# A tenth buffer for expert weights, loaded during the scan, in place of most of the room for GpSimd's DMA descriptors

## The chip, the cores and the metric

The kernel runs as one launch on one core of a Trainium2 chip. The metric is the device time of that launch in microseconds (us). TensorE is called PE, VectorE DVE, ScalarE ACT, GpSimd POOL and SyncE SP.

## The reference

Two blocks follow each other on 256 tokens of width 1024, all in float32. The first block has two layers, each of a mixer (retention, dilated attention, spatial gating) and a gated FFN. The second block is a state-space scan with a pooling branch and then a mixture of 32 experts (4 groups of 8), of which each token uses two. Cut to what matters here:

```
def hybrid_layer(...):                                   # twice
    z = jnp.matmul(rms_norm(x, g_mix_pre), w_in)
    y = concatenate([retention, dilated attention, spatial_gating(gelu(gu), gelu(gv), w_s, b_s)])
    x = x + rms_norm(jnp.matmul(y, w_out), g_mix_post)
    gate, up = jnp.split(jnp.matmul(rms_norm(x, g_ffn_pre), w_gate_up), [FFN_HIDDEN], axis=-1)
    return x + rms_norm(jnp.matmul(jax.nn.silu(gate) * up, w_down), g_ffn_post)

# second block: modulate, ssd_scan, pooling branch, post_norm, then
def hier_moe(h, lp):
    lg = hf @ lp['w_rg'] + lp['b_rg']                    # router: groups
    le = jnp.einsum('td,gde->tge', hf, lp['w_re']) ...   # router: experts of a group
    def swiglu(xb, wg, wu, wd):
        return (jax.nn.silu(xb @ wg) * (xb @ wu)) @ wd   # for all 32 experts' tokens
```

## The kernel before, in words

Each engine has one instruction stream written out by hand, and semaphores order the streams. `at(...)` gives the semaphore and count at which a named event has happened.

**Weights of the dense stages.** Weights stream through `ring` in units, which SP loads in order (`load_to`, `load`). The ring has four slots of a megabyte in the first block and two in the second. A unit is cut into quarters. Each quarter is split into a high part (ACT, `split_hi`) and a low part, made by DVE or by POOL (`lo_to`, one TENSOR_TENSOR into `split_r`); PE then multiplies with both. There are four places for split quarters, so ACT starts quarter k when PE has finished quarter k-4. In the gate/up stage of the first block's FFN (22 units, m = 0 to 21, two quarters each) DVE makes the low parts of first quarters and POOL those of second quarters. SP may load a new unit into a slot once the high and low parts of what lay there are made.

**POOL's loop in gate/up.** For each m it runs `lo_to` for the quarters ahead, then `low(m)` (the low part of the activations, after ACT has made the high part of unit m), and in the first layer one step of the generator `small_loads`. That generator issues small DMA loads for the second block; its last ten steps (m = 7 to 16) load the router's weights into WR: for each of two halves of the rows, one load from `w_router_group_2` and four from `w_router_expert_2`. In each of the ten, every one of 128 partitions has four separate runs (of 16 or 32 bytes).

**POOL's other loads.** At the start: positions, six small rows, then `conv_w`, `b_ada`, GCOL and BCOL (`ln1_g_2`, `ln1_b_2`, two runs in each partition), BP (`b_ada_2`, four runs in each partition), and then `cst1` (1344 KB). In each layer: WS (`w_s`, four runs of 512 bytes in each partition), then two rows of gains broadcast over the partitions. Later the context CX, with two runs in each partition.

**Room for POOL's descriptors.** Loads that POOL issues have lists (descriptors) that POOL writes into SBUF. The program sets aside bytes of each partition for them, 16384 by default; `kernel()` builds with the default.

**Experts.** The experts' stage streams 96 matrices of 2 MB (gate, up and down of 32 experts), numbered k = 0 to 95. They go through nine places of SLOT = 4096 floats per partition (`expert_slots`: four in `arena`, four in `ring`, one in `rows`); matrix k takes place k mod 9. Pairs of experts p share six matrices: two gates, two ups, two downs. Matrices 0 to 7 are issued by ACT as the dense stages let go of the memory, 8 and on by SP (`expert_loads`), in order; from k = 9 each waits until PE has finished with matrix k-9. Some (2, 9, 10 and 92 to 95) are loaded in two halves. Between the scan and this stage lie the gates, branches a and b and `out2`.

The lines touched are 317 to 375 (allocation and semaphores), 534 to 596 (places and loads of experts), 991 (PE's wait for the router's weights), 1768 to 1810 (ACT's expert loads), 2766 to 2772 (`small_loads`), 2790 (WS), 2888 (BP), 2990 to 3022 (SP's loads) and 3088 (`kernel()`).

Of the kernel before, what the change touches and what calls it, by code (L numbers as in the profile page):

```python
# [291 lines left out]
def program(nc, A, out):  # L292
    st = ExitStack()
    with st:
# [24 lines left out]
        posi = sb("posi", [P, 2], I32)  # L319
        rope = sb("rope", [P, 2, 2, 32])  # L320
        rt = rows[:, 4 * D:4 * D + P].rearrange("p (a b c) -> p a b c", a=2, b=2)
        posf = sb("posf", [P, 2])
        cnt = sb("cnt", [P, 1], I32)
        AR = 26624
        ar_at = nc.sbuf_base + (-nc.sbuf_base) % 32
# [46 lines left out]
        s_last = {e: sem(f"last_{e}") for e in ("dve", "pool")}  # L372
        s_w = [[sem(f"expert{i}") for i in range(9)]] + [[sem(f"expert{r}_{i}") for i in range(8)] for r in range(1, ROUNDS)]
        s_second = [sem(f"expert_second{i}") for i in range(4)]
        s_round = [None] + [{e: sem(f"round{r}_{e}") for e in ("pe", "act", "dve")} for r in range(1, ROUNDS)]
# [55 lines left out]
        GT2 = view(23424, 2, 512)  # L431
        JUNK = view(25472, 2, 512)
        ACH = view(4096, 22, 256, rounded=True)
        ACL = view(9728, 22, 256, rounded=True)
# [53 lines left out]
        def blocks8(a0, a1, rounded=False):  # L488
# [43 lines left out]
        SEL, RK, CW, RS, CM, CB = R(400, 2, 32), R(464, 2, 32), R(528, 2, 32), R(592, 2, 32), R(656, 1, 2), R(660, 2, 36)  # L532
        expert_slots = [ar[:, 18432:18432 + SLOT], ar[:, 22528:22528 + SLOT], ar[:, 10240:10240 + SLOT], ar[:, 14336:14336 + SLOT],
                        ring[:, 0:SLOT], ring[:, SLOT:2 * SLOT], ring[:, 2 * SLOT:3 * SLOT], ring[:, 3 * SLOT:4 * SLOT], rows[:, D:D + SLOT]]

        slot_for = lambda r, k: expert_slots[k % (9 if r == 0 else 8)]

# [49 lines left out]

        in_halves = lambda r, k: r == 0 and (k in (2, 9, 10) or k >= 92)

        def half_load(e, k, q):  # L590

            p, j = divmod(k, 6)
            o = slot_for(0, k)[:, q * RAW:(q + 1) * RAW]
            w = A["w_expert_up_2" if j < 4 else "w_expert_down_2"][0, 2 * p + j % 2]
            src = w.rearrange("(q p k) n -> q p (k n)", q=2, k=4)[q] if j < 4 else w.rearrange("(p q k) n -> q p (k n)", q=2, k=2)[q]
            e.dma_start(o, src).then_inc(*landed(s_second[k % 4] if q else s_w[0][k % 9], ("ew", 0, k, q)))

        def tensor(t):  # L600
# [346 lines left out]
            def convolution():  # L947
# [17 lines left out]
                for m in range(24):  # L965
                    c = CHUNKS[m]
                    if m < 3:
                        finished(m + 1)
                    else:
                        bk = take(("cv", m), ("conv", m))  # L970
                        chunk(bk if c < 20 else bk[:, 256:512], q0 + 1 + m, 0 if c < 20 else 1, 2).then_inc(*sig(s_mm, ("cv", m), ("split_done", q0 + 1 + m)))
                    if m >= 2:
                        to_tokens(m - 2)
                    if m == 1:
                        bk = take(("dtt",), ("dtraw",))
                        t.wait_ge(*at("cv", -1, "kept"))
                        for i in range(4):
                            made = t.transpose(bk[:, i * 64:(i + 1) * 64], DTT[:, tok(i)], ident[0:64, 0:64])
                        made.then_inc(*sig(s_turn, ("dtt",)))
                    if m == 10:  # L980
                        dt_sums()
                    if m == 11:
                        bk = take(("acst",), ("acsr", 0), ("acsr", 1))
                        t.wait_ge(*at("acs"))
                        for i in range(4):
                            made = t.transpose(bk[:, tok(i)], ACS[:, i % 2, :], ident)
                        made.then_inc(*sig(s_turn, ("acst_t",)))
                    if m == 17:
                        bk = take(("sct",), ("sct", "kept"))
                        t.wait_ge(*at("ab"))  # L990
                        t.wait_ge(s_small[5], 32)
                        t.wait_ge(s_small[6], 128)
# [405 lines left out]
        def scalar(s):  # L1398
# [356 lines left out]
            def gates():  # L1755
                n0 = first["u",][1]
                for u in range(2):
# [4 lines left out]
                    if u == 0:  # L1762
                        s.wait_ge(*at("y", 15))
                        for k in range(2):
                            s.dma_start(PW_(4 * k, 4), A["pool_w_2"][0].rearrange("g (k p) d -> p (g k) d", p=P)[:, 4 * k:4 * k + 4, :]).then_inc(
                                *landed(s_pw[k], ("pw_in", k)))
                        s.wait_ge(*at("mb", 31))
                        expert_load(s, 0, 0)
                s.wait_ge(*at("u", 1, 1))
# [4 lines left out]
                s.wait_ge(*at("sacc", 15))  # L1774
                expert_load(s, 0, 1)
                s.wait_ge(*at("ss", "kept"))
# [15 lines left out]
                for u in range(4):  # L1792
                    for a in range(2):
                        hi_to(n0 + 2 * u + a + 4)
                    if u >= 2:
                        s.wait_ge(*at("ba", 3))
                        half_load(s, 2, u - 2)
# [4 lines left out]
                expert_load(s, 0, 3)  # L1802
                s.wait_ge(*at("bb", 3, "kept"))
                expert_load(s, 0, 5)
                for n in range(1, 5):
                    s.wait_ge(*at("lo", len(quarters) - n))
                expert_load(s, 0, 4)
                s.wait_ge(*at("o2", 1))
                expert_load(s, 0, 6)
                expert_load(s, 0, 7)  # L1810

            def routing():
# [903 lines left out]
        def gpsimd(g):  # L2716
# [34 lines left out]
            def small_loads():  # L2751
# [14 lines left out]
                for q in range(2):  # L2766
                    rows_of = lambda x: x[512 * q:512 * q + 512].rearrange("(p k) n -> p k n", k=4)
                    g.dma_start(WR[:, 4 * q:4 * q + 4, 0:4], rows_of(A["w_router_group_2"][0])).then_inc(*landed(s_small[5]))
                    yield
                    for k in range(4):  # L2770
                        g.dma_start(WR[:, 4 * q:4 * q + 4, 4 + 8 * k:12 + 8 * k], rows_of(A["w_router_expert_2"][0, k])).then_inc(*landed(s_small[6]))
                        yield

            def layer(l):
# [9 lines left out]
                for k in range(28):  # L2784
                    lo_to(n0 + k + 4)
                    if k == 1:
                        g.wait_ge(*at("z", l, 0, 1))
                        g.wait_ge(*at("hl", j, 1, 1))
                        g.wait_ge(*at("hh", j, 1, 1))
                        g.dma_start(WS[:, :, :], A["w_s"][l].rearrange("g t s -> t g s")).then_inc(*landed(s_ws, ("ws_in", l)))  # L2790
                    if k == 4:
# [94 lines left out]
            for o, name in ((GCOL, "ln1_g_2"), (BCOL, "ln1_b_2")):  # L2886
                g.dma_start(fold(o, 2), A[name][0].rearrange("(q p k) -> p q k", q=2, k=4)).then_inc(*landed(s_col[3]))
            g.dma_start(fold(BP, 4), A["b_ada_2"][0][3 * D:5 * D].rearrange("(u p k) -> p u k", u=4, k=4)).then_inc(*landed(s_col[3], ("bp_in",)))
            layer(0)
# [73 lines left out]
        def sync(y):  # L2963
# [25 lines left out]
            def expert_loads(r, first_one):  # L2989

                n_slots = len(s_w[r])
                for k in range(first_one, 96):
                    if k >= n_slots and not (r == 0 and k in (9, 10)):
                        b, i = divmod(k - n_slots, 6)
                        y.wait_ge(*(at("gu", r, b, i // 2) if i < 4 else at("oe", r, b, 1)))
                    if not in_halves(r, k):
                        expert_load(y, r, k)
                    elif k == 10:
                        for q in range(2):
                            y.wait_ge(*at("gu", 0, 0, 0 if q else "first"))  # L3000
                            for x in (9, 10):
                                half_load(y, x, q)
# [5 lines left out]
            for l in range(2):  # L3008
# [5 lines left out]
                for m, u in ADA_AT[l].items():  # L3014
# [84 lines left out]
```

## Time and profile before

| what | value |
|---|---|
| median of 3 runs | 1635.37 us (1634.31 to 1642.18) |
| span of the profiled execution | 1635.8 us |
| PE busy | 1585.8 us (97%), 9881 matmuls |
| DVE, ACT, POOL busy | 762.6, 611.0, 473.7 us |
| DMA moved | 397.87 MB, mean 243 GB/s |
| DMA issued by POOL | 3024 packets, 9.95 MB |
| chain that ended last | PE 82%, DMA 9%, DVE 3%, ACT 2%, issue 2%, POOL 1% |

The profile describes one execution on the chip. The span runs from its first to its last instruction, and it differs from the median time by 0.4 us, so what lies around it is too small to see. Matmuls overlap, and the end of each is modelled, so PE at 97% doesn't mean that each of its instructions is at its peak. A DMA's landing is counted from the start of the issuing instruction to the last increment of its semaphore. The mean DMA share of a stretch can be a little over 1, since packets overlap.

### The profile page before, as it was taken

How to read it: one execution, taken by the hardware profiler on the slowest of the kernel's cores; microseconds unless marked ns; L12 is line 12 of the kernel's file. 1: busy time of each engine (PE TensorE's matmuls, PEld its weight loads, DVE VectorE, ACT ScalarE, POOL GpSimd, SP SyncE). 2: the span in 40 equal slices, each digit the busy share in tenths (PEclk: the TensorE clock that was granted, in tenths of full speed). 3: DMA queues.
4: the chain of work that ended last, by engine and by line, in shares of the span. 5: the costliest groups of instructions: out<-in, count | busy, mean ns of one | idle time of the engine just before them, and what ended most of it. 6: DMA issues, size and time to landing. Idle time of an engine off the chain costs nothing.

```text
span 1635.8 us, 24320 instructions
## 1 busy us (share of the span) xinstructions
PE 1585.8 (97%) x9881; PEld 1204.8 (74%) x9881; DVE 762.6 (47%) x1261; ACT 611.0 (37%) x1113; POOL 473.7 (29%) x305
## 2 busy tenths in 40 slices
PE   6999999999999999999999999999999999999997
PEld 5988899878889998888778888898644444444442
DVE  4554433246454332578776666446532323333223
ACT  4644444345544443555446665333211111111010
POOL 4342655433434444300036665343300000000000
PEclk9999999999999999999999999999999999999998
DMA  7654997546439986433313333957999999999995
GB/s 264 220 158 128 266 260 232 174 141 218 153 98 312 263 269 220 118 80 85 103 52 104 104 103 120 296 152 264 360 400 423 425 420 422 424 422 424 421 422 210
DMA packets 244757, 397.87 MB, mean 243 GB/s; under 512 B 6837, under 2 KB 195697, under 8 KB 223392
## 3 DMA queue, kind: packets, MB, share of 16 engines
q1 hardware_dynamic: 237840, 365.45, 64.6%
q10 hardware_dynamic: 3776, 20.85, 3.2%
q0 software_dynamic: 3024, 9.95, 1.8%
q8 instruction: 81, 1.33, 0.3%
q14 instruction: 36, 0.29, 0.1%
HBM read 395.17 MB, written 1.05 MB: 242 GB/s over the span
## 4 chain that ended last, share of the span: by engine, by line
PE 82%; DMA 9%; DVE 3%; issue 2%; ACT 2%; POOL 1%; ACTq 0%; DVEq 0%; POOLq 0%; SPq 0%
PE ps L145 80%; DMA arena<-in_w_expert_up 4%; DMA arena<-in_w_expert_gate 4%; PE ps L147 2%; DVE arena L151 1%; DVE arena L155 1%; DMA ring<-in_w_out 1%; POOL split_r L151 1%; ACT arena L149 1%; DMA X<-in_x 1%; ACT split_r L149 1%; DVE split_r L151 0%; DMA ring<-in_w_in 0%; POOL arena_r L151 0%; DVE X L155 0%
## 5 line engine op out<-in xcount | busy, mean ns | idle before, releaser
L145 PE MATMUL ps<-arena_r,split_r 128*128 128x256 f32 (+1 forms) x2984 | 459.9, 288 | 2.2 <-POOL split_r L151 2.2
L151 POOL TENSOR_TENSOR split_r<-ring,split_r 128x1024 fp32r<-128x1024 f32 (+1 forms) x142 | 329.3, 2320 | 304.2 <-ACT split_r L149 275.6
L145 PEld LDWEIGHTS ps<-arena_r,split_r 128*128 128x128 f32 x2984 | 393.3, 188 | 19.7 <-issue 13.6
L149 ACT ACTIVATE split_r<-ring 128x1024 fp32r<-128x1024 f32 (+1 forms) x293 | 295.7, 1019 | 265.2 <-PE ps L145 183.2
L151 DVE TENSOR_TENSOR split_r<-ring,split_r 128x1024 fp32r<-128x1024 f32 (+1 forms) x151 | 217.4, 1442 | 302.6 <-ACT split_r L149 302.4
L145 PE MATMUL ps<-split_r,arena_r 128*128 128x512 f32 (+1 forms) x1520 | 341.0, 378 | 4.1 <-POOL split_r L151 2.4
L145 PEld LDWEIGHTS ps<-split_r,arena_r 128*128 128x128 f32 x1520 | 276.1, 189 | 50.3 <-issue 7.1
L145 PE MATMUL ps<-arena 128*64 128x512 f32 (+8 forms) x1456 | 299.1, 461 | 6.3 <-DMA arena<-in_w_expert_gate 2.2
L145 PE MATMUL ps<-hhh_r,split_r 128*128 128x256 f32 (+1 forms) x976 | 221.7, 316 | 0.0
L145 PEld LDWEIGHTS ps<-arena 128*64 128x64 f32 (+2 forms) x1456 | 126.0, 148 | 129.7 <-issue 115.2
L145 PE MATMUL ps<-ring,arena 128*64 128x512 f32 (+2 forms) x768 | 211.4, 576 | 3.0 <-DMA ring<-in_w_expert_up 1.7
L149 ACT ACTIVATE arena<-ps 128x256 f32<-128x256 f32 (+4 forms) x175 | 75.4, 446 | 257.3 <-PE ps L145 215.3
L145 PEld LDWEIGHTS ps<-hhh_r,split_r 128*128 128x128 f32 x976 | 161.6, 188 | 12.5 <-issue 0.6
L151 DVE TENSOR_TENSOR arena<-arena,ps 128x512 f32<-128x512 f32 (+1 forms) x120 | 72.7, 634 | 202.9 <-PE ps L145 177.3
L145 PEld LDWEIGHTS ps<-ring,arena 128*64 128x64 f32 (+1 forms) x768 | 77.3, 144 | 98.8 <-issue 89.4
L171 POOL DMA_DIRECT2D rows<-in_ln_g x1 | 0.6, 617 | 412.2 <-PE ps L145 412.2
L149 ACT ACTIVATE arena<-ps,modc 128x128 f32<-128x128 f32 x80 | 30.0, 455 | 199.2 <-PE ps L145 198.5
L149 ACT ACTIVATE arena_r<-arena 128x512 fp32r<-128x512 f32 (+2 forms) x96 | 51.0, 540 | 138.5 <-DVE arena L155 86.9
L145 PEld LDWEIGHTS ps<-arena,X 128*128 128x128 f32 x640 | 77.4, 198 | 28.5 <-issue 26.4
L145 PE MATMUL ps<-arena,X 128*128 128x128 f32 x640 | 82.6, 284 | 14.6 <-DVE arena L153 14.6
L155 DVE SCALAR_TENSOR_TENSOR arena<-ps,rows,arena 128x508 f32<-128x508 f32 (+4 forms) x104 | 69.7, 675 | 28.5 <-ACT arena L149 21.9
L151 POOL TENSOR_TENSOR arena_r<-arena,arena_r 128x256 fp32r<-128x256 f32 (+1 forms) x46 | 38.1, 830 | 151.3 <-ACT arena_r L149 143.7
(164 smaller groups left out, 1234.0 us busy)
## 6 DMA issues: line engine op xcount, KB each, us to landing
ring<-in_w_gate_up SPq DMA_DIRECT2D x88, 512.0 KB, 7.4
arena<-in_w_expert_gate SPq DMA_DIRECT2D x15, 2048.0 KB, 27.9
ring<-in_w_in SPq DMA_DIRECT2D x57, 512.0 KB, 5.3
ring<-in_w_expert_gate SPq DMA_DIRECT2D x13, 2048.0 KB, 25.7
ring<-in_w_expert_down SPq DMA_DIRECT2D x13, 2048.0 KB, 28.5
arena<-in_w_ada SPq DMA_DIRECT2D x24, 1024.0 KB, 7.4
arena<-in_w_expert_up SPq DMA_DIRECT2D x12, 2048.0 KB, 25.1
ring<-in_w_down SPq DMA_DIRECT2D x22, 1024.0 KB, 4.9
```

The lines of the kernel that those rows point to most:

```text
L145: made = e.matmul(*a, **k)
L147: made = e.transpose(*a, **k)
L149: made = e.activation(*a, **k)
L151: made = e.tensor_tensor(*a, **k)
L155: made = e.scalar_tensor_tensor(**k)
L171: made = e.dma_start(*a, **k)
```

## The change

- The room for POOL's descriptors falls from the default of 16384 bytes to 512 bytes per partition. A new tensor `tenth` of 16 KB per partition is allocated, and `rope` (512 bytes per partition) moves into unused floats of `arena`. The bytes add up: 15872 and 512 are freed and 16384 are taken.
- `tenth` becomes place 0 of ten. Matrix k takes place k mod 10, and from k = 10 each load waits for matrix k-10. Matrices 1 to 8 are issued by ACT where it issued 0 to 7, into the same memory, and SP goes on at 9 where it went on at 8. The loads in halves become 3, 10, 11 and 92 to 95.
- Matrix 0 is issued by SP in the middle of the scan, after the eighth unit of `merged`.
- The loads of POOL with four runs in each partition are issued as two loads of two runs each: the ten loads of WR, the two of WS and the one of BP. PE's wait for WR counts twice as much.

```
-        rope = sb("rope", [P, 2, 2, 32])
+        tenth = sb("tenth", [P, SLOT])
+        rope = ar[:, 26496:26624].rearrange("p (a b c) -> p a b c", a=2, b=2)
...
-        expert_slots = [ar[:, 18432:18432 + SLOT], ar[:, 22528:22528 + SLOT], ...
+        expert_slots = [tenth[:, :], ar[:, 18432:18432 + SLOT], ar[:, 22528:22528 + SLOT], ...
-        slot_for = lambda r, k: expert_slots[k % (9 if r == 0 else 8)]
+        slot_for = lambda r, k: expert_slots[k % (10 if r == 0 else 8)]
...
-        in_halves = lambda r, k: r == 0 and (k in (2, 9, 10) or k >= 92)
+        in_halves = lambda r, k: r == 0 and (k in (3, 10, 11) or k >= 92)
...
                 for q in range(2):
                     rows_of = lambda x: x[512 * q:512 * q + 512].rearrange("(p k) n -> p k n", k=4)
-                    g.dma_start(WR[:, 4 * q:4 * q + 4, 0:4], rows_of(A["w_router_group_2"][0])).then_inc(*landed(s_small[5]))
+                    for b in range(2):
+                        g.dma_start(WR[:, 4 * q + 2 * b:4 * q + 2 * b + 2, 0:4], rows_of(A["w_router_group_2"][0])[:, 2 * b:2 * b + 2, :]).then_inc(
+                            *landed(s_small[5]))
                     yield
                     for k in range(4):
-                        g.dma_start(WR[:, 4 * q:4 * q + 4, 4 + 8 * k:12 + 8 * k], rows_of(A["w_router_expert_2"][0, k])).then_inc(*landed(s_small[6]))
+                        for b in range(2):
+                            g.dma_start(WR[:, 4 * q + 2 * b:4 * q + 2 * b + 2, 4 + 8 * k:12 + 8 * k],
+                                        rows_of(A["w_router_expert_2"][0, k])[:, 2 * b:2 * b + 2, :]).then_inc(*landed(s_small[6]))
                         yield
...
-                        g.dma_start(WS[:, :, :], A["w_s"][l].rearrange("g t s -> t g s")).then_inc(*landed(s_ws, ("ws_in", l)))
+                        for x in range(2):
+                            g.dma_start(WS[:, 2 * x:2 * x + 2, :], A["w_s"][l, 2 * x:2 * x + 2].rearrange("g t s -> t g s")).then_inc(
+                                *landed(s_ws, *([("ws_in", l)] if x else [])))
...
+            load_to(first["merged",][0] + 8)
+            expert_load(y, 0, 0)
             load_to(first["end",][0])
             y.wait_ge(*at("o2", 1, 1, "kept"))
-            expert_loads(0, 8)
+            expert_loads(0, 9)
...
-    nc = bacc.Bacc("TRN2", target_bir_lowering=False, num_devices=1)
+    nc = bacc.Bacc("TRN2", target_bir_lowering=False, num_devices=1, dynamic_dma_scratch_size=512)
```

## Rows read from the trace of the kernel before

**Rows 1.** Part 2 of the page: GB/s that the DMAs moved, in 40 slices.

```profile
GB/s 264 220 158 128 266 260 232 174 141 218 153 98 312 263 269 220 118 80 85 103 52 104 104 103 120 296 152 264 360 400 423 425 420 422 424 422 424 421 422 210
```

**Rows 2.** Busy time by stretch: us, each engine, granted clock, DMA share, GB/s.

```profile
1172.00:1200.00 28.00, 28.00 (x164) 12.78 (x162) 9.37 (x18) 5.42 (x12) 7.72 (x6) 1.00 0.89 336
1200.00:1423.00 223.00, 223.00 (x1212) 103.46 (x1210) 71.72 (x128) 29.56 (x72) 0.00 (x0) 1.00 1.01 423
1423.00:1611.00 188.00, 178.75 (x948) 84.62 (x944) 55.60 (x96) 22.78 (x55) 1.14 (x2) 1.00 1.01 422
```

**Rows 3.** Chain that ended last, from 1400 us: start, us, what.

```profile
1423.67 29.83 DMA arena<-in_w_expert_up
...
1592.89 18.24 PE ps L145 x76
```

**Rows 4.** The same chain from 180 to 270 us (gate/up, first layer).

```profile
179.94 90.09 PE ps L145 x749
```

**Rows 5.** Busy time from WR's first load to its last.

```profile
194.40:258.10 63.70, 63.70 (x532) 58.97 (x531) 24.03 (x25) 26.79 (x39) 37.95 (x30) 1.00 0.87 241
```

**Rows 6.** Groups of POOL's instructions, 194 to 259 us: busy, mean ns | idle before.

```profile
L151 POOL TENSOR_TENSOR split_r<-ring,split_r 128x1024 fp32r<-128x1024 f32 x10 | 24.1, 2408 | 0.2
L151 POOL TENSOR_TENSOR arena_r<-arena,arena_r 128x256 fp32r<-128x256 f32 x10 | 7.4, 736 | 24.9 <-ACT arena_r L149 24.9
L171 POOL DMA_DIRECT2D small<-in_w_router_expert x8 | 6.2, 770 | 0.0
```

**Rows 7.** Timeline of one gate/up unit: start, us, engine, instruction [idle before].

```profile
192.38 0.38 ACT L149 ACTIVATE arena<-ps 128x256 f32<-128x256 f32 x1 [1.76 <-PE ps L145]
...
194.43 0.79 POOL L171 DMA_DIRECT2D small<-in_w_router_group  x1
195.24 2.40 POOL L151 TENSOR_TENSOR split_r<-ring,split_r 128x1024 fp32r<-128x1024 f32 x1
```

**Rows 8.** DMA issues of POOL: KB, us to landing; WR's median, then four alone.

```profile
small<-in_w_router_expert POOLq DMA_DIRECT2D x8, 16.0 KB, 5.8
...
small<-in_w_router_group POOLq DMA_DIRECT2D x1, 8.0 KB, 4.5
...
small<-in_w_router_expert POOLq DMA_DIRECT2D x1, 16.0 KB, 6.1
...
small<-in_w_router_expert POOLq DMA_DIRECT2D x1, 16.0 KB, 3.8
...
small<-in_w_router_group POOLq DMA_DIRECT2D x1, 8.0 KB, 7.3
```

**Rows 9.** The same view, POOL's issues at 15.7, 29.3 and 361.5 us.

```profile
stat<-in_ln_g POOLq DMA_DIRECT2D x1, 4.0 KB, 2.5
...
arena<-in_w_s POOLq DMA_DIRECT2D x1, 256.0 KB, 6.5
...
arena<-in_w_s POOLq DMA_DIRECT2D x1, 256.0 KB, 7.5
```

**Rows 10.** Timeline of POOL and PE early in the first layer.

```profile
17.93 0.55 POOL L171 DMA_DIRECT2D arena<-in_cst  x1
...
25.02 4.34 POOL L151 TENSOR_TENSOR split_r<-ring,split_r 128x768 fp32r<-128x768 f32 x2 [6.55 <-ACT split_r L149]
...
34.06 1.84 POOL L151 TENSOR_TENSOR split_r<-ring,split_r 128x768 fp32r<-128x768 f32 x1 [3.95 <-ACT split_r L149]
...
37.66 4.41 PE L145 MATMUL ps<-split_r,arena_r 128*128 128x384 f32 x24
```

**Rows 11.** Timeline of POOL and PE early in the second layer.

```profile
367.73 1.88 POOL L151 TENSOR_TENSOR split_r<-ring,split_r 128x768 fp32r<-128x768 f32 x1 [5.43 <-ACT split_r L149]
...
373.30 6.49 PE L145 MATMUL ps<-split_r,arena_r 128*128 128x384 f32 x36
```

**Rows 12.** Busy time by stretch, early in the first layer and amid the scan.

```profile
30.00:60.00 30.00, 29.74 (x184) 28.43 (x183) 17.70 (x42) 15.86 (x29) 13.29 (x11) 1.00 0.90 295
...
920.00:1000.00 80.00, 80.00 (x622) 69.77 (x621) 50.38 (x102) 49.27 (x112) 49.56 (x28) 1.00 0.39 106
```

More of the change, by code:

```diff
@@ L372, in program @@
         s_last = {e: sem(f"last_{e}") for e in ("dve", "pool")}
-        s_w = [[sem(f"expert{i}") for i in range(9)]] + [[sem(f"expert{r}_{i}") for i in range(8)] for r in range(1, ROUNDS)]
-        s_second = [sem(f"expert_second{i}") for i in range(4)]
+        s_w = [[sem(f"expert{i}") for i in range(10)]] + [[sem(f"expert{r}_{i}") for i in range(8)] for r in range(1, ROUNDS)]
+        s_second = [sem(f"expert_second{i}") for i in range(5)]
         s_round = [None] + [{e: sem(f"round{r}_{e}") for e in ("pe", "act", "dve")} for r in range(1, ROUNDS)]
@@ L532, in program @@
         SEL, RK, CW, RS, CM, CB = R(400, 2, 32), R(464, 2, 32), R(528, 2, 32), R(592, 2, 32), R(656, 1, 2), R(660, 2, 36)
-        expert_slots = [ar[:, 18432:18432 + SLOT], ar[:, 22528:22528 + SLOT], ar[:, 10240:10240 + SLOT], ar[:, 14336:14336 + SLOT],
+        expert_slots = [tenth[:, :], ar[:, 18432:18432 + SLOT], ar[:, 22528:22528 + SLOT], ar[:, 10240:10240 + SLOT], ar[:, 14336:14336 + SLOT],
                         ring[:, 0:SLOT], ring[:, SLOT:2 * SLOT], ring[:, 2 * SLOT:3 * SLOT], ring[:, 3 * SLOT:4 * SLOT], rows[:, D:D + SLOT]]
-        slot_for = lambda r, k: expert_slots[k % (9 if r == 0 else 8)]
+        slot_for = lambda r, k: expert_slots[k % (10 if r == 0 else 8)]
         ADA_AT = ({4: 0, 8: 1, 12: 2, 16: 3, 20: 4}, {3: 5, 6: 6, 9: 7, 12: 8, 15: 9, 18: 10, 20: 11})
@@ L595, in half_load @@
             src = w.rearrange("(q p k) n -> q p (k n)", q=2, k=4)[q] if j < 4 else w.rearrange("(p q k) n -> q p (k n)", q=2, k=2)[q]
-            e.dma_start(o, src).then_inc(*landed(s_second[k % 4] if q else s_w[0][k % 9], ("ew", 0, k, q)))
+            e.dma_start(o, src).then_inc(*landed(s_second[k % 5] if q else s_w[0][k % 10], ("ew", 0, k, q)))
         def tensor(t):
@@ L990, in convolution @@
                         t.wait_ge(*at("ab"))
-                        t.wait_ge(s_small[5], 32)
-                        t.wait_ge(s_small[6], 128)
+                        t.wait_ge(s_small[5], 64)
+                        t.wait_ge(s_small[6], 256)
                         both = fold_columns(modc[:, 24:40, :])
@@ L1767, in gates @@
                         s.wait_ge(*at("mb", 31))
-                        expert_load(s, 0, 0)
+                        expert_load(s, 0, 1)
                 s.wait_ge(*at("u", 1, 1))
@@ L1774, in gates @@
                 s.wait_ge(*at("sacc", 15))
-                expert_load(s, 0, 1)
+                expert_load(s, 0, 2)
                 s.wait_ge(*at("ss", "kept"))
@@ L1796, in gates @@
                         s.wait_ge(*at("ba", 3))
-                        half_load(s, 2, u - 2)
+                        half_load(s, 3, u - 2)
                     s.wait_ge(*at("mt", u))
@@ L1801, in gates @@
                 s.wait_ge(*at("bb", 3))
-                expert_load(s, 0, 3)
+                expert_load(s, 0, 4)
                 s.wait_ge(*at("bb", 3, "kept"))
-                expert_load(s, 0, 5)
+                expert_load(s, 0, 6)
                 for n in range(1, 5):
                     s.wait_ge(*at("lo", len(quarters) - n))
-                expert_load(s, 0, 4)
+                expert_load(s, 0, 5)
                 s.wait_ge(*at("o2", 1))
-                expert_load(s, 0, 6)
                 expert_load(s, 0, 7)
+                expert_load(s, 0, 8)
             def routing():
@@ L2887, in gpsimd @@
                 g.dma_start(fold(o, 2), A[name][0].rearrange("(q p k) -> p q k", q=2, k=4)).then_inc(*landed(s_col[3]))
-            g.dma_start(fold(BP, 4), A["b_ada_2"][0][3 * D:5 * D].rearrange("(u p k) -> p u k", u=4, k=4)).then_inc(*landed(s_col[3], ("bp_in",)))
+            for x in range(2):
+                g.dma_start(fold(BP, 4)[:, 2 * x:2 * x + 2, :], A["b_ada_2"][0][(3 + x) * D:(4 + x) * D].rearrange("(u p k) -> p u k", u=2, k=4)).then_inc(
+                    *landed(s_col[3], *([("bp_in",)] if x else [])))
             layer(0)
@@ L2992, in expert_loads @@
                 for k in range(first_one, 96):
-                    if k >= n_slots and not (r == 0 and k in (9, 10)):
+                    if k >= n_slots and not (r == 0 and k in (10, 11)):
                         b, i = divmod(k - n_slots, 6)
@@ L2997, in expert_loads @@
                         expert_load(y, r, k)
-                    elif k == 10:
+                    elif k == 11:
                         for q in range(2):
                             y.wait_ge(*at("gu", 0, 0, 0 if q else "first"))
-                            for x in (9, 10):
+                            for x in (10, 11):
                                 half_load(y, x, q)
```

## The prediction

> **What bounds the kernel now.** I read the DMA rate over the span first [rows 1]. It moves between 52 and 312 GB/s up to the 28th of 40 slices, and from the 31st on it stands at 420 to 425: there the experts' weights come in, and nothing else in the span has such a flat top. The stretches by engine say which engine pays for that [rows 2]. From 1172 to 1200 us PE never stands and the DMA share is 0.89. From 1200 to 1423 PE is busy all the time too, with the DMA at 1.01. From 1423 to 1611 the DMA share is still 1.01, but PE is busy for 178.75 of 188.00 us. So PE first lives on what was loaded ahead, runs out of it at 1423, and then waits for transfers, 9.25 us in all. The chain of waits agrees: its first long piece of DMA begins at 1423.67, and the last matmuls after the last such piece begin at 1592.89 [rows 3]. In the experts' stage the end is set by the DMA queue: so many matrices of 2 MB at one rate.
>
> Before the experts the bound is another. In the gate/up stage of the first layer the chain is one piece of PE, 90.09 us with 749 matmuls [rows 4], and in WR's part of it PE is busy for 63.70 of 63.70 us [rows 5]. There a load costs nothing as long as the low parts of the weights, half of which POOL makes, are ready ahead of PE.
>
> **The change part by part.**
>
> *The tenth place.* A matrix is 1024 x 512 floats, 2.097 MB, and at 423 GB/s [rows 2] it takes 4.96 us of the queue. With matrix 0 already in `tenth`, the nine others take the places that the nine of before took, at the same events, and the first refill (10 in place of 9) is released by the same matmuls. From there 86 matrices are to come instead of 87. The hole in the queue between 1172 and 1200 (share 0.89) comes from places that are not yet free and stays as it was. The queue ends 4.96 us earlier, and PE can follow, since it has 9.25 us of waits to give. Gain: 5.0 us. Its ends are 0 (if something else ended the stage) and 9.25 (all of PE's waits).
>
> *Matrix 0 amid the scan.* One more transfer of 5 us on SP's queue, where the DMA share is 0.39 at 106 GB/s [rows 12]. It stands behind the unit just sent, and the next unit is only asked for about 10 us later (1 MB per unit at 106 GB/s), when the transfer is over. Cost 0, cover: the idle 0.61 of the queue; without it 5 us at most.
>
> *Places in another order, halves of 3, 10 and 11, `rope` moved, twice the count in PE's wait.* These are the same instructions at other addresses and numbers: 0.
>
> *POOL's smaller room.* This is the part with a price. Only loads with four runs in each partition are cut in two; those with two runs (GCOL, BCOL, CX) stay whole. So I read the diff as saying that 512 bytes hold a list of two runs but not one of four. Then two halves, which are one whole, don't fit together either. POOL has to stand at the second half until the room of the first is free, and nothing else on POOL runs meanwhile. The trace of before has no such wait, since the room is 32 times as large. Bounds for it: 0 if the room is free when the list has been taken, and the whole time to landing if it is free on completion. I take landing, for the semaphore that counts it is the only sign of a load's progress that this program has. Landing took 3.8 to 7.3 us in WR's loads, median 5.8 [rows 8]. A load of GCOL's kind landed in 2.5 us at the start, and WS's in 6.5 and 7.5 us [rows 9].
>
> For WR, let L1 and L2 be the times to landing of the halves. One turn of POOL's loop was low 0.74 + load 0.77 + split 2.41 = 3.92 us of work in a period of 63.7 / 10 = 6.37 us, with 2.49 us idle [rows 5, 6]. In the new turn the first half is issued, POOL stands until it has landed (L1), issues the second (0.77), splits (2.41), does `low` (0.74), and can issue the next first half only when the second has landed. A turn is thus L1 + max(3.92, L2). The split that waits behind it is due soon. In the unit that PE ended at 192.38, the low part was ready at 195.24 + 2.40 = 197.64 [rows 7]. A unit has 48 matmuls, at 90.09 / 749 = 0.120 us each 5.8 us [rows 4], so a quarter takes 2.9. The part is used three quarters after 192.38, at 201.1: slack 3.5 us once, not for each unit. What POOL's ten turns take beyond 63.7 + 3.5 = 67.2 us goes straight to PE.
> - Least: L1 = L2 = 3.8 gives ten turns of 7.72, 77.2 us, a loss of 10.0.
> - Most: 5.8 for both gives 11.6, 116 us, a loss of 48.8.
> - Taken: L1 = 4.8, midway, for the first half is issued 0.8 us after the split whose end lets SP send the next megabyte; L2 below 3.92, because that burst is over by then and the turns are longer than before, so the queue is less full. Ten turns of 8.72 are 87.2 us: a loss of 20.0.
>
> By the Trainium skill (DMA: Bandwidth & Descriptors, Anatomy of one DMA) a DMA of POOL costs about 2.0 us plus its bytes at 436 GB/s; by that a half would land in about 2 us, the turn would be 5.9 us and nothing would be lost. The trace speaks against it in this stage, with 3.8 us at least and 5.8 in the median [rows 8], while at 15.7 us it comes near, with 2.5 [rows 9].
>
> *The other halves.* At the start the order is GCOL, BCOL, BP, BP, and three of them stand for a predecessor, 3 x (2.5 - 0.77) + 0.77 = 6.0 us. POOL ended its loads at 18.48 and its first split began at 25.02 after 6.55 us idle [rows 10], so the split moves by nothing. The load of `cst1`, 1344 KB or 3.2 us of the queue, moves from 17.9 into the stretch where the share is 0.90 [rows 12] and PE takes splits almost as they come. Cost 0 to 3, taken 1. WS in the first layer holds POOL from 29.31 for 6.5 + 0.77 us, to 36.6. The split of 34.06 then ends at 38.4, and the matmuls that use it as their second quarter start 2.2 us after 37.66 [rows 9, 10]: 0. In the second layer it holds POOL to 369.8, so the split of 367.73 ends at 371.7, before PE's 373.30 [rows 9, 11]: 0.
>
> *Sum.* -5.0 + 0 + 20.0 + 1 = +16. The profiled execution (span 1635.8) is 0.4 us from the median, so the sum is added to the median: 1635.4 + 16 = 1651.
>
> **The rivals.**
> - *POOL doesn't stand, since the room is free as soon as the list is taken.* For it: the issue itself takes only 0.77 us [rows 6], and the halves add ten times 0.77 us to turns with 2.49 idle. Against it: the list has to stay until the DMA engines have read it, and WR's data landed 3.8 us and more after the issue. Time: 1635.4 - 5.0 = 1630.4. This is the case on the other side, not slower.
> - *POOL stands, but halves land fast.* The cost begins only where ten turns pass 67.2 us, so at L1 = 6.72 - 3.92 = 2.8 us. GCOL's 2.5 us would do [rows 9]; none of the four loads of WR shown comes under 3.8 [rows 8]. A half writes half of the runs, and WR's landing may be mostly that. Time: 1630.4 to 1632, taken 1631. The rule of the Trainium skill cited above, about 2.0 us for a small DMA, would lead here.
> - *The tenth place doesn't do what it is there for*, because matrix 0 hits the scan's units or the holes in the queue before 1200 grow by what was saved, and the halves cost nothing. Then nothing is won: 1635. The DMA share of 0.39 in the scan speaks against it.
> - *It gives more than one matrix.* If the spread of landings, not the rate, made PE's waits, a matrix more in hand could take all 9.25 us: 1626. The flat 1.01 after 1200 [rows 2] speaks against it.
>
> **How the numbers follow.** Chances: the forecast's case 0.66; no standing 0.14; short standing 0.12; nothing won 0.04; more won 0.04. The forecast's case by itself runs from 1635.4 - 5 + 10 = 1640 to about 1670; its far end 1635.4 - 5 + 48.8 + 3 = 1682 would need every half to take the median of before, although the queue is then less full. The range has to hold the two cases near 1630 as well, which have 0.26: 1629.5 to 1668. What this kernel's measurement can tell from no change is about 0.5%, 8.2 us. Slower by more than that (over 1643.6) needs a loss of 12.2 us or more, an L1 of 4.02: about 0.56 of the 0.66. The rest of it, 0.10, and the cases at 1630 to 1635, 0.30 together, are within 0.5%. Only the last case is faster by more than 0.5%: 0.04.
>
> **What would show each step.** The tenth place: the experts' stretch with the DMA share at 1.01 ends 5 us nearer to its start, PE's first wait there comes two or three pairs later, and its waits fall from 9.25 to about 4.3 us. POOL's room: the second of each pair of WR's loads starts some 4 to 5 us after the first, or it lasts that long, POOL has no idle time before `low`, and PE waits for `split_r` from POOL in that stage, with 20 us in sum, where it had none. If the pairs stand 0.8 us apart with POOL idle as before, the forecast is wrong and 1630 is right. The scan: ACT's waits for `in_w_in` there don't grow. What would make it wrong otherwise: a landing of the halves under 2.8 us, or a delay at the start that PE can't hide.

## The result

| | before | after |
|---|---|---|
| median | 1636.3 us (4 runs) | 1669.7 us (4 runs, 1665.4 to 1671.5) |
| span of the profiled execution | 1635.8 us | 1669.6 us |
| ratio, after to before | | 1.019, 95% interval 1.0173 to 1.0208 |

The change makes the kernel 33.5 us slower. The forecast was slower, but by 16 us, and 1669.7 lies 1.7 us above the range. The lines of the page that changed most: the share of POOL and of issue in the chain that ended last, and the granted clock, which was at full speed in these slices before.

```profile
span 1669.6 us, 24333 instructions
...
PE 1600.7 (96%) x9881; PEld 1216.8 (73%) x9881; DVE 769.3 (46%) x1261; ACT 611.9 (37%) x1113; POOL 486.8 (29%) x318
...
PEclk9999988999999999999999999999999999999999
...
PE 79%; DMA 7%; POOL 4%; issue 4%; DVE 4%; ACT 2%; SPq 0%; ACTq 0%; DVEq 0%; POOLq 0%
```

Where the time went is told by a comparison of the two traces instruction by instruction. DVE has the same 1517 instructions, those of its queue included, in the same order in both, so the start of the n-th in after less its start in before is the shift at that place (times are those of before):

```
at, us            31    61    184 to 210  230    251    271 to 363  384 to 1038  1144 to 1453  1499   1541   end
shift, us, after  +1.2  +6.5  +6.2        +19.0  +31.8  +40.1       +42.1        +38.7         +36.3  +34.0  +33.8
```

So the pieces are: +6.4 in the first 61 us, +33.9 in WR's stretch, +2.0 early in the second layer, nothing through the scan, -3.3 at `out2`, and -4.9 in the experts' stage.

The piece of 33.9 by stretch and by POOL's groups. First the busy time of the engines by stretch (us, PE, PEld, DVE, ACT, POOL, granted clock, DMA share, GB/s), then what POOL did from 194 to 300 us (busy, mean ns | idle time before), then PE's waits over the whole span:

```profile
194.00:300.00 106.00, 85.00 (x619) 78.53 (x618) 30.80 (x31) 33.00 (x47) 54.73 (x45) 0.89 0.62 176
920.00:1000.00 80.00, 80.00 (x614) 68.91 (x612) 48.09 (x98) 47.99 (x108) 47.91 (x28) 1.00 0.47 132
1240.00:1500.00 260.00, 260.00 (x1406) 120.40 (x1403) 83.96 (x149) 33.91 (x82) 0.00 (x0) 1.00 1.01 423
1500.00:1645.00 145.00, 140.19 (x750) 65.60 (x749) 43.45 (x76) 18.50 (x45) 1.14 (x2) 1.00 1.01 422
...
L151 POOL TENSOR_TENSOR split_r<-ring,split_r 128x1024 fp32r<-128x1024 f32 x12 | 28.5, 2377 | 0.2
L151 POOL TENSOR_TENSOR arena_r<-arena,arena_r 128x256 fp32r<-128x256 f32 x12 | 13.9, 1162 | 4.2 <-ACT arena_r L149 4.2
L171 POOL DMA_DIRECT2D small<-in_w_router_expert x16 | 11.7, 731 | 39.4 <-issue 24.7 <-PE ps L145 14.7
L171 POOL DMA_DIRECT2D small<-in_w_router_group x4 | 2.9, 734 | 9.5 <-issue 5.7 <-PE ps L145 3.9
...
PE ps L145 <- POOL split_r L151: 23.2, 11, 5.1
```

Against [rows 5]: PE was busy for all of the stretch, and now for 85.0 of 106.0 us. Against [rows 6]: POOL's idle time stood before `low` (24.9 us, waiting for ACT); now 48.9 us stand before the loads of WR and 4.2 before `low`. Against [rows 2]: in the experts' stage PE stands for 4.81 us (145.00 - 140.19) where it stood for 9.25.

One turn of POOL's loop, with the start, the time taken and in brackets the idle time before:

```profile
218.03 1.75 POOL L151 TENSOR_TENSOR arena_r<-arena,arena_r 128x256 fp32r<-128x256 f32 x1
219.74 0.74 POOL L171 DMA_DIRECT2D small<-in_w_router_expert  x1
225.80 0.72 POOL L171 DMA_DIRECT2D small<-in_w_router_expert  x1 [5.32 <-PE ps L145]
226.54 2.35 POOL L151 TENSOR_TENSOR split_r<-ring,split_r 128x1024 fp32r<-128x1024 f32 x1
228.84 1.75 POOL L151 TENSOR_TENSOR arena_r<-arena,arena_r 128x256 fp32r<-128x256 f32 x1
...
small<-in_w_router_expert POOLq DMA_DIRECT2D x1, 8.0 KB, 5.8
...
small<-in_w_router_expert POOLq DMA_DIRECT2D x1, 8.0 KB, 2.1
```

The first half is issued at 219.74 and the second only at 225.80, after 5.32 us in which POOL does nothing. The last two lines are the landings of this pair: the first half took 5.8 us from issue to landing and was down at 225.5, and the second was issued 0.3 us later and landed in 2.1 us. All ten pairs do this: the second half is issued 0.3 or 0.4 us after the first has landed.

### The profile page after: what moved, and what is told of

Read it like the earlier page. It is cut to its first block, busy times and chain, and to the rows that moved or that the text cites. A ratio compares the mean times of both kernels' runs of the same rounds, so it can differ in the third digit from the quotient of the medians.

```text
span 1669.6 us, 24333 instructions
## 1 busy us (share of the span) xinstructions
PE 1600.7 (96%) x9881; PEld 1216.8 (73%) x9881; DVE 769.3 (46%) x1261; ACT 611.9 (37%) x1113; POOL 486.8 (29%) x318
## 4 chain that ended last, share of the span: by engine, by line
PE 79%; DMA 7%; POOL 4%; issue 4%; DVE 4%; ACT 2%; SPq 0%; ACTq 0%; DVEq 0%; POOLq 0%
PE ps L145 77%; DMA arena<-in_w_expert_gate 2%; DMA arena<-in_w_expert_up 2%; POOL split_r L151 2%; PE ps L147 2%; DVE arena L151 1%; POOL arena_r L151 1%; POOL small L171 1%; DVE arena L155 1%; ACT arena L149 1%; DMA ring<-in_w_in 1%; ACT split_r L149 1%; DMA X<-in_x 1%; DMA ring<-in_w_out 1%; DVE split_r L151 1%
## 5 line engine op out<-in xcount | busy, mean ns | idle before, releaser
L145 PE MATMUL ps<-arena_r,split_r 128*128 128x256 f32 (+1 forms) x2984 | 472.6, 293 | 22.7 <-POOL split_r L151 22.6
L145 PEld LDWEIGHTS ps<-arena_r,split_r 128*128 128x128 f32 x2984 | 404.5, 194 | 41.7 <-issue 33.4
L145 PE MATMUL ps<-arena 128*64 128x512 f32 (+8 forms) x1392 | 319.1, 455 | 2.3 <-DMA ring<-in_w_expert_gate 1.0
L145 PEld LDWEIGHTS ps<-split_r,arena_r 128*128 128x128 f32 x1520 | 277.6, 190 | 48.1 <-issue 5.3
L145 PE MATMUL ps<-ring,arena 128*64 128x512 f32 (+2 forms) x688 | 225.3, 574 | 2.0 <-DMA rows<-in_w_expert_gate 1.2
L145 PEld LDWEIGHTS ps<-arena 128*64 128x64 f32 (+2 forms) x1392 | 129.9, 149 | 117.1 <-issue 102.0
L151 POOL TENSOR_TENSOR arena_r<-arena,arena_r 128x256 fp32r<-128x256 f32 (+1 forms) x46 | 43.4, 944 | 125.2 <-ACT arena_r L149 117.4
```

The costliest lines, as they stand in the source:

```text
L145: made = e.matmul(*a, **k)
L151: made = e.tensor_tensor(*a, **k)
```

## The experiments

Nine kernels ran, beside runs of the kernel before on the same chips. The theory (A): the room of 512 bytes doesn't hold two halves, and POOL stands at the second until the first has landed. The rivals: the extra issues or the load in the scan are what costs (B, C, D).

**e1_room_alone**: the small room and the halves, without the tenth place.

```
 # on the kernel before, beside the loads of WR, WS and BP in halves
-    nc = bacc.Bacc("TRN2", target_bir_lowering=False, num_devices=1)
+    nc = bacc.Bacc("TRN2", target_bir_lowering=False, num_devices=1, dynamic_dma_scratch_size=512)
```

> The kernel before with the room for descriptors at 512 bytes and POOL's loads in halves, but nine places for experts and no load in the scan. Theory A (POOL stands at the second half until the first has landed, because the room is full): all of the loss without the gain of the tenth place. In the changed kernel the shift against before was +6.4 us at the start, +33.9 in WR's stretch, +2.0 early in the second layer, -3.3 near out2 and -4.8 in the experts' stage, so this one should be 38 us (34 to 42) slower than before. Rival B (the load in the scan, the tenth place or the moved tensors carry a good part): less than 25 us slower. It also tells whether the -3.3 comes with the room or with the tenth place.

Measured: 1674.3 us against 1636.6, ratio 1.0223 (1.0202 to 1.0244), 37.7 us slower. The shift is +6.3 at 61 us, +39.5 after WR and +40.8 at 1184; in the experts' stage it stays (+40.7 at the end). PE's waits for POOL's splits:

```profile
PE ps L145 <- POOL split_r L151: 25.4, 12, 5.0
```

The whole loss comes with the room; rival B falls. The -3.3 at `out2` is here too (-3.4), without the tenth place.

**e2_halves_alone**: the same halves, with the full room.

```
 # e1, but with the default room:
     nc = bacc.Bacc("TRN2", target_bir_lowering=False, num_devices=1)
```

> The kernel before with POOL's loads in halves, and the full room of 16384 bytes. Theory A: the second half is issued at once after the first, 0.72 us more in a turn with 2.49 us idle, so the time is that of before within 2 us. Rival C (the 13 more issues, or their colliding with DVE's operations, carry the loss): 10 us or more slower.

Measured: 1634.9 us, ratio 0.9996 (0.9983 to 1.0009). POOL's groups from 193 to 259 us (busy, mean ns | idle before):

```profile
L171 POOL DMA_DIRECT2D small<-in_w_router_expert x16 | 11.5, 723 | 0.0
L151 POOL TENSOR_TENSOR arena_r<-arena,arena_r 128x256 fp32r<-128x256 f32 x11 | 8.1, 739 | 22.2 <-ACT arena_r L149 22.2
```

Sixteen issues at 0.72 us with no idle time before them, and 22.2 us left idle before `low`. Rival C falls: halves cost nothing, standing does.

**e3_room_1024**: as e2, with 1024 bytes.

```
 # e2, but with
+    nc = bacc.Bacc("TRN2", target_bir_lowering=False, num_devices=1, dynamic_dma_scratch_size=1024)
```

> The kernel before (nine places) with POOL's loads in halves issued back to back, and a room of 1024 bytes, twice that of the change. Theory A (what counts is whether the lists of the halves that haven't landed fit together): a pair fits with half of the next, and a pair landed within 6.5 us where it was issued back to back, so nearly nothing stands and the time is that of the kernel before within 4 us. Rival E (any room that is small makes POOL wait for each load, or the cost falls in proportion to the room): 10 us or more slower.

Measured: 1646.5 us against 1637.8, ratio 1.0055 (1.0036 to 1.0073): 8.7 us slower, between the two expectations. Eight of the ten pairs are issued back to back and two stand:

```profile
208.67 0.73 POOL L171 DMA_DIRECT2D small<-in_w_router_expert  x1
214.95 0.72 POOL L171 DMA_DIRECT2D small<-in_w_router_expert  x1 [5.55 <-issue]
...
219.71 1.45 POOL L171 DMA_DIRECT2D small<-in_w_router_expert  x2
```

The pair before had been issued at 201.63 and had landed by 208.1, before this one began; the second half waited for its own first half (landed at 214.6), though two halves fit here. The other pair that stands, at 245.11 and 251.03, does the same. So a room that has run out makes POOL wait also for the newest load, and not only for as much room as it needs. Why it ran out at these two, the third and the eighth of the ten, is open. That the cost isn't in proportion to the room is shown: the stretch lost 6.6 us here and 32 in e1.

**e4_spread**: the changed kernel, a half of WR in each step.

```
                     for k in range(4):
                         for b in range(2):
                             g.dma_start(WR[...], ...)
-                        yield
+                            yield
...
                 for k in range(18):                # down stage
                     lo_to(n0 + k + 4)
+                    if l == 0:
+                        next(loads, None)
```

> The changed kernel with one of WR's twenty halves in a step of POOL's loop instead of two; the last five go to the steps of the down stage. The room stays at 512 bytes. Theory A: a half finds its predecessor landed or nearly so (landings of 4.3 to 7.0 us for the first halves, a step of 5.8 us or more, slack of 3.5 us once), so the 33.9 us of WR's stretch fall to 0 to 6, and the rest stays: 6.4 + 2.0 - 3.3 - 4.8, about the time of before, 1634 to 1643 us. Rival C (each half costs, standing or not): 1650 us or more.

Measured: 1641.7 us against 1636.6, ratio 1.0031 (1.0016 to 1.0046). The shift stays at +6.1 from 184 to 278 us, through what was WR's stretch: the 33.9 us are gone with the same number of halves in the same room. It then rises by 3.9 in the down stage, where two steps hold one split:

```profile
295.17 0.73 POOL L171 DMA_DIRECT2D small<-in_w_router_expert  x1
301.07 0.72 POOL L171 DMA_DIRECT2D small<-in_w_router_expert  x1 [5.17 <-issue]
301.82 2.42 POOL L151 TENSOR_TENSOR split_r<-ring,split_r 128x1024 fp32r<-128x1024 f32 x1
```

**e5_nothing_stands**: beside that, the other halves and the loads after them in steps of their own.

```
-                    if k == 4:                     # projection: rows of gains, both
+                    if k in (1, 4):                # WS, a half in each
...
+                    if k in (7, 9):                # rows of gains, one in each
...
+                    if k in (14, 16, 18, 20) and l == 0:
+                        next(late)                 # GCOL, BCOL, BP, BP
-                    if k == 8 and l == 0:
+                    if k == 12 and l == 0:         # rows for MG
```

> The same, and the halves of GCOL, BCOL, BP and WS, the rows of gains and the rows for MG are also issued in different steps of POOL's loop in the first layer's (and second layer's) projection, so that none finds the room full. Theory A: only the tenth place is left, 5 us faster than before, 1629 to 1633 us. Rival D (cst1 and the load in the scan cost by themselves, or POOL's splits collide with DVE's rotary products wherever the loads are put): 1635 us or more.

Measured: 1633.1 us, ratio 0.9984 (0.9973 to 0.9996). The shift is -0.3 from 61 to 278 us, so the start has nothing left of its 6.4, but the down stage adds 4.3, near the 3.9 of e4. The time is at the upper end of what theory A gave, and with nothing left at the start rival D falls.

**e6_even_steps**: the last five halves of WR in every second step of the down stage.

```
-                    if l == 0:
+                    if l == 0 and k % 2 == 0:
                         next(loads, None)
```

> The run in which nothing was to stand, once more, with the last five halves of WR in every second step of the down stage. There they had stood for 5.2 and 4.4 us, since two steps hold only one split of POOL, and PE had lost 4.3 us. Theory A: these 4.3 us come back, 1628 to 1630 us, 7 to 8 us under what the kernel before has on the same chip if its last stages gain 5 us from the tenth place and the rest is chance. Rival D (the loss in the down stage is of the load in the scan or of more issues): 1633 us as before.

Measured: 1629.3 us against 1637.8, ratio 0.9951 (0.9935 to 0.9968). The halves of the down stage no longer stand:

```profile
290.62 0.73 POOL L171 DMA_DIRECT2D small<-in_w_router_expert  x1
...
296.01 0.73 POOL L171 DMA_DIRECT2D small<-in_w_router_expert  x1 [0.51 <-issue]
...
301.06 0.73 POOL L171 DMA_DIRECT2D small<-in_w_router_expert  x1
```

This version is faster than both kernels. Against the kernel before it gains 8.5 us in the medians. Of that the trace shows 4.9 in the experts' stage (shift -3.5 at 1184 and at 1453, -8.4 at the end). The other 3.6 us aren't explained. In the traces they come from stretches where before was slow (`out2` above all), but that is one execution of before and says nothing of its median.

**e7_pair_later** and **e9_pair_after_fill** ask why the first half lands late.

```
                     low(m)
+                    if l == 0 and 7 <= m < 17:
+                        g.wait_ge(*at("hi", k))    # e7: k, the quarter that POOL splits next
...
                     low(m)
+                    if l == 0 and 7 <= m < 17:
+                        ...
+                        then(g.memset(tenth[:, 0:3072], 0.0), ("fill", m))    # e9, instead
```

> The changed kernel, with one more wait in POOL's loop ahead of each of WR's ten pairs: for the high part that the next split needs anyway. The pair is issued about 3.2 us later after the last split, with whose end SP's next megabyte starts. Theory F (the first half lands late, after 5.5 us, since it is queued behind that megabyte; the second lands in 2.2 us because it comes after it): the first half lands in 2 to 3 us, a turn is 4.0 + 2.5 + 0.72 + 2.4 = 9.6 us, as long as the 9.8 of the changed kernel, and the time is within 6 us of 1670. Rival G (the first half's landing is a fixed cost of a load issued after an arithmetic instruction, or after an idle stretch): it still lands in 5.5 us, a turn is 12.6 us, and the time is near 1695.

Measured: 1667.4 us against 1637.8, ratio 1.0171 (1.0148 to 1.0195). It settles nothing: the wait was over before POOL came to it, and the load still follows `low` without a gap (229.46 + 1.75, then 231.17):

```profile
229.46 1.75 POOL L151 TENSOR_TENSOR arena_r<-arena,arena_r 128x256 fp32r<-128x256 f32 x1
231.17 0.74 POOL L171 DMA_DIRECT2D small<-in_w_router_expert  x1
235.69 0.72 POOL L171 DMA_DIRECT2D small<-in_w_router_expert  x1 [3.79 <-issue]
```

> The changed kernel, with a fill of 3072 floats per partition of the tenth place by POOL ahead of each of WR's ten pairs (work that is not part of the computation). The wait that was to put the pair off didn't do so, since its event had come before. Let D be the time of the fill, 1 to 3 us. The pair is issued D later after the split that lets SP send its next megabyte. Theory F (the first half is queued behind that megabyte): its landing, 5.5 us on the mean in the changed kernel, falls by about D, down to the 2.2 us of the second halves at the least, and a turn stays at 9.8 us or rises by less than D/3; WR's stretch costs 34 to 44 us. Rival G (the landing is a fixed cost of a POOL load issued at this place): the landing stays at 5.5 us, a turn rises by D, and the stretch costs 34 + 10 D.

Measured: 1678.2 us against 1640.1, one run of each. SP loads matrix 0 after the last fill here. The fill took 2.66 us. Over the ten pairs the time from the first half's issue to the second's fell from a mean of 5.54 us (changed kernel: 4.6, 6.0, 6.1, 4.8, 4.6, 6.4, 4.7, 6.2, 4.9, 7.3) to 4.00 (2.8, 5.7, 4.3, 2.5, 2.4, 6.7, 2.9, 3.9, 2.5, 6.6), and WR's stretch cost 41.0 us. One turn:

```profile
231.07 1.75 POOL L151 TENSOR_TENSOR arena_r<-arena,arena_r 128x256 fp32r<-128x256 f32 x1
232.77 2.65 POOL L165 MEMSET tenth<- 128x3072 f32 x1
235.37 0.74 POOL L171 DMA_DIRECT2D small<-in_w_router_expert  x1
237.84 0.72 POOL L171 DMA_DIRECT2D small<-in_w_router_expert  x1 [1.74 <-issue]
```

Theory F gave 34 to 44 and rival G 61 for the stretch: rival G falls. The fall is 1.5 us in the mean, less than the 2.66 us of the fill. Pair by pair, the five of 4.6 to 4.9 us became 2.4 to 2.9, while three stayed at 5.7 to 6.7. These three (issued at 211.81, 253.91 and 296.17) are the ones that come 6.2 to 6.4 us after SP's two loads of `w_ada`, 2 MB; no run takes those loads away.

**e8_ws_apart**: e4 with WS's halves apart, and cst1 still late.

```
 # e4 with
+                    if k in (1, 4):                # WS, a half in each
+                    if k in (7, 9):                # rows of gains
+                    if k == 12 and l == 0:         # rows for MG
```

> The run with WR's halves in steps of their own, and beside it WS's two halves three steps of the projection apart, with the rows of gains in the steps after them. GCOL, BCOL and BP still stand for each other at the start, so cst1 is still issued 7 us late. Theory H (the 6.4 us at the start come from WS's wait: POOL then runs two splits on end, behind which DVE's rotary product and PE's transposes stand): the shift at the start falls from +6.3 to +1 or less, and the time from 1641.7 to about 1636. Rival I (they come from cst1's load, moved among those of w_in): the shift stays at 4 us or more.

Measured: 1635.2 us, ratio 0.9990 (0.9975 to 1.0004). The shift at 61 us is +2.1 instead of +6.3, a little over the 1 that theory H named; rival I falls. What happened at the start is seen in the lines of the changed kernel, then of this one, then of the kernel before:

```profile
37.13 5.28 DVE L151 TENSOR_TENSOR arena<-arena 128x192 f32<-128x192 f32 x4
37.20 0.72 POOL L171 DMA_DIRECT2D arena<-in_w_s  x1 [5.90 <-PE ps L145]
37.94 3.58 POOL L151 TENSOR_TENSOR split_r<-ring,split_r 128x768 fp32r<-128x768 f32 x2
...
41.80 1.56 PE L147 MATMUL ps<-cst_sb,arena 128*128 128x128 f32 x6 [3.36 <-DVE arena L151]
```

```profile
36.02 1.84 POOL L151 TENSOR_TENSOR split_r<-ring,split_r 128x768 fp32r<-128x768 f32 x1 [3.96 <-ACT split_r L149]
37.05 1.96 DVE L151 TENSOR_TENSOR arena<-arena 128x192 f32<-128x192 f32 x4
...
39.05 0.82 PE L147 MATMUL ps<-cst_sb,arena 128*128 128x128 f32 x6
```

```profile
35.47 1.58 DVE L151 TENSOR_TENSOR arena<-arena 128x192 f32<-128x192 f32 x4
```

In the changed kernel POOL stands for WS's second half until 37.20 and then runs two splits on end, 37.94 to 41.5. DVE's four rotary products, begun at 37.13, take 5.28 us in that time, where they took 1.58 before and 1.96 in this run, and PE's transposes wait for them until 41.80. By the Trainium skill (SBUF — State Buffer, Who interferes with whom) a VectorE instruction with two inputs in SBUF and a GpSimd instruction that reads SBUF exclude each other, and the one that comes second waits for the whole of the other. These rows agree: 5.28 us beside two splits, against 1.58 and 1.96. In e1 and e4 there are 0.9 and 0.8 us between the two splits, and PE stands for DVE's products all the same, 3.5 and 3.6 us.

## Why the prediction was right and wrong

- **What bounds the kernel** held. The experts' stage is set by the queue: with one matrix fewer to come it ended earlier by 4.9 us in after and by 4.9 to 5.2 in e5 to e9, and by 0.2 or less in e1, e2 and e3, which have nine places. In e4 it was 3.3: one matrix landed late there, and PE stood 2.5 us for it. The term was -5.0. PE's waits there were to fall to about 4.3 us and fell to 4.81. One reading was loose: the chain's DMA piece begins at 1423.67, where the load is issued, but PE stands for the first time at 1453.6. In after it does so at 1567.2, which is 75 us later at the shift of 38.7, the two or three pairs that were forecast.
- **Matrix 0 amid the scan: 0**, held. The shift is +42.1 at 405 us and +41.9 at 1038.
- **The reading of the diff** (two halves don't fit in the room; POOL stands until the landing; nothing else runs meanwhile) held, and both rivals near 1630 us fell: the second issue starts 0.3 us after the first half's landing, and e2, e4 and e1 leave nothing else. Slower than before was right.
- **WR's term was mis-sized: 20.0 taken, 33.9 measured.** Three numbers in it were off.
  - L1 was taken as 4.8 us, below the 5.8 of the rows, since the queue would be less full. It was (share 0.62 against 0.87 [rows 5]), but from one half's issue to the other's it is 5.54 us in the mean. e9 shows most of what the step missed: it isn't the mean load of the queue that slows the first half but what SP has just sent. As the split ends, SP sends a megabyte, and the first half follows 0.5 to 2.6 us later. For the half issued at 219.74 it is this one:

```profile
218.17 0.99 SPq L171 DMA_DIRECT2D ring<-in_w_gate_up  x2
```

  In three of the turns it also comes 3 to 5 us after the two megabytes of `w_ada`, and in two of these the landing is over 6 us. The row of the median [rows 8] was the better value. Ten times 0.74 is 7 us.
  - The work between the halves of one turn and the next was taken as 3.92 us and was 4.41 (nine turns of 87.8 us less nine waits of 48.1, by nine). `low` has a mean of 1.16 us against 0.74 [rows 6], with 1.75 where DVE's split runs beside it (217.05 to 219.2 in after, `low` from 218.03), and in the last pair the first half stood for 0.82 us too, until the second half before it had landed. That is 5 us in ten turns. The sum priced POOL's instructions by rows in which they ran beside others than they would.
  - The ten turns take 98.9 us (200.6 to the end of `low` at 299.5) and so explain 98.9 - 67.2 = 31.7 us. 2 us are left. They can be the slack, which was an estimate from one unit, or the clock: PE's granted clock was 0.89 over this stretch, after it began to stand, where it was 1.00. Neither was tried.
- **The start: 1 taken, 0 to 3 allowed, 6.4 measured.** The price was put on the late load of `cst1`, which costs 2.1 at most (e8), and WS's wait was costed at nothing, since the delayed split would be ready 1.5 us ahead of PE. That cover held for the split alone. It left out that POOL catches up on two splits with hardly a gap, and that DVE needs its port for the product on which PE's transposes wait. That made PE stand for 3.36 us, and 1.2 us of the 6.4 were there at 31 us, ahead of it. Most of the rest goes with the clock, which the prediction didn't price: from 42 to 48 us it is a mix of its two levels, 2.4 and 1.2 GHz, after PE has stood, while e8 has 1.00 throughout. The 24 matmuls that took 4.41 us [rows 10] took 5.15 in after and 6.48 in e4, where the clock was lower still. The stretches of after, first the start and then the second layer:

```profile
36.00:42.00 6.00, 2.64 (x17) 2.32 (x16) 5.90 (x6) 1.69 (x2) 4.78 (x4) 1.00 0.76 242
42.00:48.00 6.00, 6.00 (x28) 5.74 (x27) 5.16 (x12) 1.83 (x3) 0.57 (x2) 0.72 1.01 345
412.00:418.00 6.00, 5.00 (x21) 4.76 (x22) 5.63 (x12) 1.14 (x3) 1.70 (x3) 0.72 0.96 281
```

  The same two places in e4:

```profile
42.00:48.00 6.00, 6.00 (x23) 6.00 (x23) 4.18 (x9) 1.28 (x2) 0.00 (x0) 0.60 0.90 309
382.00:388.00 6.00, 5.30 (x32) 5.07 (x33) 5.69 (x13) 1.83 (x3) 1.38 (x3) 1.00 0.94 311
```

- **The second layer: 0 taken, +2.0 measured.** WS's wait there is 5.6 us and PE stands 3.2 us for DVE's products, but in before it already stood 2.9 us for them at this place. What differs is the clock behind that: 1.00 in before, 0.72 in after. In e4 WS's wait (5.5) and PE's (3.1) are those of after, the clock stays at 1.00 (last line above), and the shift rises by 0.2 only. In e3, where WS doesn't wait, PE stands 2.5 us, the clock is 0.50 from 380 to 386 us, and the shift rises by 2.3. So most of the 2.0 goes with the clock. Why it falls after one stand and not after another is open.
- **The sum.** The -3.3 us at `out2` are in all nine other kernels too (-2.5 to -3.8), with either number of places, so the tenth place doesn't make them. The chains of before and then of after show a slower load of `w_out` in before, and behind it 36 matmuls that took longer; the granted clock was 0.86 from 1139 to 1151 us in before and 1.00 at that place in after:

```profile
1129.19 6.24 DMA ring<-in_w_out
...
1139.08 10.21 PE ps L145 x36
```

```profile
1170.59 4.91 DMA ring<-in_w_out
...
1179.20 8.66 PE ps L145 x36
```

  That this is chance of the one profiled execution of before is likely and not shown: all nine kernels also have POOL's loads in halves, but e2, with the halves alone, is less than 2.8 us faster than before (the end of its interval). 6.4 + 33.9 + 2.0 - 3.3 - 4.9 = 34.1, against 33.8 between the spans.
- **The range** missed by 1.7 us. Its upper end was drawn at 1668 although the bounds of the terms reached 1682, on the word that every half would need the median of before. The first halves came near it (5.25 us from issue to landing in the mean); the second halves didn't need it. Against the forecast, WR's term missed by 13.9 us, the start by 5.4 and the second layer by 2.0, and the 3.3 at `out2`, which wasn't forecast, took some of that back.

## What to carry to other kernels

A small room for GpSimd's descriptors turns each of its loads into a possible stand of the whole engine, for as long as the load before needs to land; with a step of other work between the loads the same room cost nothing here (e4 in WR's stretch, e6). When a DMA's landing becomes a term, take it from rows at the same place in the cycle of the other queues, not from the mean load. And when an engine is held up, price also what it does when it is let go: work caught up in one piece collides with engines that shared its port in turns, and the engine that stood for it may go on at a lower clock.

## What the runs showed of the hardware that was not expected

- POOL, out of room, waited for the newest load as well: with 1024 bytes a second half stood for 5.55 us until its own first half had landed, though the two fit back to back in the other eight pairs (e3).
- The landing of a load of 8 KB from POOL went from 2.1 to 7.0 us with what SP had sent just before it; put off by 2.66 us, the five that had taken 4.6 to 4.9 us took 2.4 to 2.9 (e9). The Trainium skill (DMA: Bandwidth & Descriptors, Anatomy of one DMA) gives about 2 us for a small DMA of POOL; the runs agree for loads issued when the queue had drained (2.0 to 2.2 us), and not for those behind a burst.
- The granted clock fell from 1.00 to 0.89 over a stretch in which PE was busy for 85.0 of 106.0 us. One stand of 3.36 us was followed by 0.72 over the next 6 us (after, from 42 us); a stand of 3.1 or 3.2 us in the second layer was followed by 0.72 in after and by 1.00 in e4. Where the clock was lower, the same 24 matmuls took 5.15 and 6.48 us instead of 4.41.
